# Moving two 128x320 products of a recurrent layer from VectorE to GpSimd, with a new wait on ScalarE

## What is computed

```
y_a = (on + bonus) * silu(g_rwkv)          # silu(g) = g * sigmoid(g)
on  = (o - mean) * rsqrt(var + eps) * ln_w + ln_b
```

## Time and profile before

| | us |
|---|---|
| median of 3 runs | 1145.81 |
| lowest, highest | 1145.09, 1146.93 |
| the profiled execution, its time | 1146.05 |
| the profiled execution, its span | 1144.5 |

### The profile page before, as it was taken

How to read it: one execution, slowest core, us unless ns; L and a number is a source line. 1 busy time by engine, 2 the same in 40 slices (tenths; PEclk the granted TensorE clock), 3 DMA queues, 4 the chain that set the end, 5 groups by cost and what they waited for, 6 DMA issues and landing times.

```text
span 1144.5 us, 23678 instructions
## 1 busy us (share of the span) xinstructions
PE 1117.6 (98%) x8594; PEld 1072.2 (94%) x8594; DVE 794.6 (69%) x1681; ACT 543.7 (48%) x960; POOL 159.7 (14%) x273
## 2 busy tenths in 40 slices
PE   5999999999999999999999999999999999999998
PEld 5889998999999999999999999999999999989998
DVE  5979897979798888988678544444444497685442
ACT  5444747566574747474643333333333343354342
POOL 2422131314131221221140000000000500000000
PEclk9999999999999999999999999999999999999999
DMA  9714433434343343443464555555555965516551
GB/s 239 199 38 124 122 104 111 113 110 115 110 128 97 107 127 99 115 121 103 129 184 130 152 147 154 153 144 149 147 148 147 283 186 148 149 54 167 168 161 38
DMA packets 279708, 155.10 MB, mean 136 GB/s; under 512 B 7717, under 2 KB 275661, under 8 KB 279012
## 3 DMA queue, kind: packets, MB, share of 16 engines
q1 hardware_dynamic: 272528, 139.65, 43.6%
q0 software_dynamic: 6992, 14.87, 4.9%
q10 hardware_dynamic: 148, 0.04, 0.0%
HBM read 149.15 MB, written 5.61 MB: 135 GB/s over the span
## 4 chain that ended last, share of the span: by engine, by line
PE 70%; DVE 17%; issue 6%; DMA 4%; ACT 3%; DVEq 0%; SPq 0%; ACTq 0%; POOL 0%; POOLq 0%
PE acc L1753 14%; PE acc L1755 13%; PE acc L1754 13%; PE wide L1755 6%; PE wide L1754 6%; PE wide L1753 6%; PE wide L1777 4%; DVE wl L1116 3%; PE wide L1860 2%; PE wide L2157 2%; DVE rn L1221 1%; PE wide L1772 1%; DMA wraw<-in_w_out 1%; ACT wh L719 1%; DVE kkn L1511 1%
## 5 line engine op out<-in xcount | busy, mean ns | idle before, releaser
L1116 DVE TENSOR_TENSOR wl<-wraw,wh 128x1024 fp32r<-128x1024 f32 x256 | 315.8, 1240 | 168.6 <-ACT wh L719 166.5
L719 ACT CAST wh<-wraw 128x1024 fp32r<-128x1024 f32 x256 | 266.8, 1048 | 213.3 <-PE acc L1755 124.0
L1753 PE MATMUL acc<-hh,wh 128*128 128x320 f32 (+1 forms) x1084 | 349.4, 322 | 8.6 <-DVE rS L1132 5.6
L1754 PE MATMUL acc<-hl,wh 128*128 128x320 f32 (+1 forms) x1084 | 336.5, 310 | 0.0
L1755 PE MATMUL acc<-hh,wl 128*128 128x320 f32 (+1 forms) x1084 | 335.8, 310 | 0.0
L1753 PEld LDWEIGHTS acc<-hh,wh 128*128 128x128 f32 x1084 | 204.2, 188 | 13.1 <-issue 7.4
L1754 PEld LDWEIGHTS acc<-hl,wh 128*128 128x128 f32 x1084 | 204.1, 188 | 0.3
L1755 PEld LDWEIGHTS acc<-hh,wl 128*128 128x128 f32 x1084 | 204.1, 188 | 0.0
L1753 PE MATMUL acc<-x1h,wh 128*128 128x320 f32 x256 | 81.0, 316 | 0.0
L1753 PE MATMUL acc<-mh,wh 128*128 128x320 f32 x256 | 79.4, 310 | 0.2 <-DVE wl L1116 0.2
L1755 PE MATMUL acc<-x1h,wl 128*128 128x320 f32 x256 | 79.1, 309 | 0.0
(11 more groups left out here) (424 smaller groups left out, 2003.7 us busy)
## 6 DMA issues: line engine op xcount, KB each, us to landing
wraw<-in_w_in SPq DMA_DIRECT2D x160, 512.0 KB, 3.8
wraw<-in_w_branch SPq DMA_DIRECT2D x32, 512.0 KB, 4.0
wraw<-in_w_out SPq DMA_DIRECT2D x32, 512.0 KB, 4.3
wraw<-in_w_ple_gate SPq DMA_DIRECT2D x32, 512.0 KB, 4.2
xt<-in_x_prompt SPq DMA_DIRECT2D x2, 1024.0 KB, 7.2
S0n<-in_state_wkv POOLq DMA_DIRECT2D x64, 32.0 KB, 3.6
out<-so POOLq DMA_DIRECT2D x16, 128.0 KB, 4.1
xt<-in_x_prompt POOLq DMA_DIRECT2D x2, 1024.0 KB, 7.8
```

Source lines behind the costliest of these rows:

```text
L719: A.copy(wh[:, slot, :], wraw[:, slot, :]).then_inc(s["hi_ready"], 1)
L1116: V.tensor_tensor(wl[:, slot, :], wraw[:, slot, :], wh[:, slot, :].bitcast(F32), ALU.subtract).then_inc(s["lo_ready"], 1)
L1753: M.matmul(out[:, 0:width], wh[:, slot, wcol], hi, start=first, stop=False)
L1754: M.matmul(out[:, 0:width], wh[:, slot, wcol], lo, start=False, stop=False)
```

## The change

The product y (L1521) and the product sg (L1305) leave VectorE's queue and are done by GpSimd. On GpSimd sg stands ahead of the copy cur_n and y ahead of the waits for the stores' landing, with a wait for each. ScalarE's second exponential, which overwrites dO, waits until sg is done (and so until the y before it is done), and VectorE's bU, which overwrites sgt, waits for sg.

```diff
 (GpSimd, mix)
                 wait_alone("cur_m_ready", r + 1)
                 wait_alone("acc_free", r * TILES_STEP + (ACC_STEP + TILES_STEP))
+                wait_alone("sg_ready", r + 1)
+                gp_.tensor_tensor(sg[:, :], sgt[:, :], gS[:, :], ALU.mult).then_inc(s["sgs_ready"], 1)
                 gp_.tensor_copy(cur_n[:, :], par[:, LN_W * PAIRS:(LN_B + 1) * PAIRS].rearrange("p (n q) -> p n q", q=PAIRS)
 (GpSimd, mix_out, behind the stores)
+                wait_alone("dve_step", r * 3 + 3)
+                gp_.tensor_tensor(yf[:, ds(r * T, T)], dO[:, :], sg[:, :], ALU.mult).then_inc(s["y_done"], 1)
+
                 wait_alone("eout", r * 32 + 32)
                 wait_alone("sout", r * 32 + 32)
+                wait_alone("y_done", r + 1)
 (ScalarE, mix)
                 A.activation(pi[:, :], cl[:, :], ACT.Exp, scale=DECAY).then_inc(s["exp_ready"], 1)
+                act.wait_ge(s["sgs_ready"], r + 1)
                 A.activation(pd[:, :], cl[:, :], ACT.Exp, scale=-DECAY).then_inc(s["exp_ready"], 1)
 (VectorE, start of mix)
-                dve.wait_ge(s["sg_ready"], r + 1)
                 dve.wait_ge(s["acc_free"], r * TILES_STEP + (ACC_STEP + TILES_STEP))
-                V.tensor_tensor(sg[:, :], sgt[:, :], gS[:, :], ALU.mult).then_inc(s["sgs_ready"], 1)
 (VectorE, ahead of bU)
+                dve.wait_ge(s["sgs_ready"], r + 1)
 (VectorE, end of mix)
-                dve.wait_ge(s["dve_step"], r * 3 + 3)
-                dve.wait_ge(s["sgs_ready"], r + 1)
-                V.tensor_tensor(yf[:, ds(r * T, T)], dO[:, :], sg[:, :], ALU.mult).then_inc(s["y_done"], 1)
                 out(5)
```

## The result

The changed kernel takes 1160.16 us (median of 4 runs, 1159.23 to 1160.24) against 1145.45 us (4 runs, 1144.85 to 1146.93) before: ratio 1.0125, 95% interval 1.0107 to 1.0142. It is slower, by 14.7 us in the medians. The forecast was 1158.3 us, with a range of 1151.0 to 1163.5. Every line after L603 has another number than before: y is L648, sg L603, pd L861, sq_l L1321, rS L1139.

A forecast was written before the change was run, and what follows sets the result against it. TensorE, busy 98% of the span, was taken to wait at pair boundaries for VectorE's queue. Six boundaries at +2.19 us (+13.1), with -0.4 and -0.2 at the ends, gave +12.5: 1158.3 us, range 1151.0 to 1163.5.

The forecast's parts named there:

- What bounds the kernel: At pair boundaries TensorE waits for VectorE's queue up to rS; each us shorter gives up to 0.95 us a pair.
- without a pause of note: From the pair's boundary to rS, VectorE was said to work with no notable idle time.
- The new order at the boundary: Pair r = 4: y holds kf, sg follows cur_p and waits for wl, pd follows sg; sq_l 2.19 us later.
- The size of a boundary: Each of six boundaries (r = 1 to 6) costs 2.19 us more, +13.1 us together.
- the straight line: GpSimd's 128x320 product takes 0.74 us, between 423 ns for 128 columns and 1048 ns for 512.
- the loop's turn: On GpSimd between y and cur_p, an estimated 0.2 us beside the waits.
- The ends: First pair (r = 0) -0.4 us, last pair (r = 7) -0.2, last y 0, at most +0.5.
- the sum: Six boundaries and the ends together cost +12.5 us, giving 1158.6 against the profiled execution, so 1158.3 us.
- sg gets in before wl: Rival at the boundary, chance 0.18 including no exclusion: +1.11 us a pair, 1151.9 us; without exclusion +1.44, 1153.9.
- the relief of VectorE comes through: Rival, chance 0.06: sg done early enough, the 0.95 us gap before tile 3 goes at six boundaries, 1139.5 us.
- The signs: Pairs r = 1 to 6: late sg, VectorE idle before sq_l, TensorE waiting for sq_l, rS wait staying near 0.8 us.
- The collision rule: VectorE instructions with two SBUF inputs and GpSimd instructions reading SBUF exclude each other; the first to start keeps the port pair.

The follow-up runs named there:

- the kernel with y late: Against the kernel before: both products on GpSimd, sg early behind the stores' issue, y mid next pair, dO in xp1, no ScalarE wait; 1139.24 us, ratio 0.9946.
- the kernel above with y at the boundary: Against the kernel before: both products on GpSimd, sg early behind the stores' issue, y at the boundary, ScalarE waits for y alone; 1144.24 us, ratio 0.9993.

## Why the prediction was right, and where it was off

- **What bounds the kernel**: right. TensorE waits for VectorE's queue between the boundary and rS; lengthening it by 2.52 us a boundary cost 2.56 us a pair, shortening it gave 0.89 (the kernel with y late). The words "without a pause of note" pass over one pause of 0.54 us in the kernel before, in which VectorE waits with the wl at 337.56 for ScalarE's cast wh. That cast stands behind bBD, which waits for VectorE's bU, so it comes earlier or later with VectorE's queue.
- **The new order at the boundary**: right in every step. y held kf, cur_p came behind y and sq, sg was dispatched just behind wl (0.28 us, foreseen 0.33) and was held by it; pd followed sg, and sq_h and sq_l followed pd.
- **The size of a boundary**: 2.56 instead of 2.19 us. Three terms were too small by 0.13 us each: y began 0.28 us after the dO step, not 0.15, which was VectorE's own distance; a product took 0.87, not the 0.74 of the straight line; sg ended 0.74 behind wl, not 0.61. One was too large, the step from sg to pd (0.03 instead of 0.1). Together +0.32, which is the difference of 2.52 to 2.19 but for 0.01. The 0.2 us for the loop's turn had no row behind it: from y's end to cur_p it took 0.72 us instead of 0.63, which made no difference, since cur_p ended behind sq, and sg behind wl, all the same. The estimate from the Trainium skill ("GPSIMD Engine Reference", section 3.1 Elementwise), 0.97 us, was 0.10 too high, where the straight line was 0.13 too low.
- **The ends**: the first pair was not 0.4 us quicker. From VectorE's first scan to kf it took 4.98 us (77.45 to 82.43) instead of 4.83 (78.94 to 83.77): sg, done early there (0.87 us from 78.24), met VectorE's pm product (1.15 instead of 0.49 us), and zr (from 80.70) met t_l (1.26 instead of 0.49). Around the last pair VectorE's and ScalarE's order was as foreseen; from gp to gp it took 59.31 us instead of 59.09.
- **Against the profiled executions** the sum is 13.2 us (1157.7 to 1144.5), with 12.5 foreseen, but this is closer than the terms deserve: the profiled execution of the changed kernel reached its first scan 1.5 us sooner, at 77.45 us. This point moves between 77.13 and 80.07 from kernel to kernel in the traces of the study, and what runs ahead of it is not touched by the change. The medians, 14.7 us apart, are the better measure. The forecast lies 1.9 us below the measured median, and the six boundaries alone cost 2.2 us more than forecast (15.3 against 13.1).
- **The rivals.** That sg gets in before wl was tried with the wait ahead of wl: it gives 1.0078, a loss still. Forecast were 1151.9 to 1153.9 us, 6.1 to 8.1 over the median of before; measured were 9.2 over it (1153.43 to 1144.27), a little more than its price. That the relief of VectorE comes through didn't happen in the change, but does in the kernel with y late. Against that rival the prediction put the chain on GpSimd at 2.6 us without a collision; its own terms, with 0.2 us for an undisturbed cur_p, add up to 3.1 (0.74, 0.63, 0.2, 0.79, 0.74), which speaks against it the more.
- **The signs.** sg's end 4.64 us after gp's start (4 to 4.5 foreseen, so a little late), VectorE's idle time 3.89 (3 to 4), TensorE's wait for sq_l 1.79 (1 to 2): right. The wait for rS stayed near 0.8 where it appears, but it appears four times and not seven; the last section says why.
- **The collision rule**: the Trainium skill ("SBUF — State Buffer", section Who interferes with whom) is borne out: kf, sq, sq_l, ar, the scan and wl, each with two inputs in SBUF, were drawn out or drew out a GpSimd instruction. That gp, with one input in PSUM, stays out of y's way can't be read from the changed kernel: they overlap for 0.12 us only, and y, held until gp's end, would have ended 0.74 us behind it, where it did end (0.75). Two rows of the kernel before show such a pair, a VectorE product with one input in PSUM and a GpSimd copy inside its time, each at its own length:

```profile
282.49 0.48 DVE L1385 TENSOR_TENSOR ARK<-wide,cm 128x320 f32<-128x320 f32 x1
```

```profile
282.60 0.22 POOL L554 COPY cur_m<-par 128x14 f32 x1
```

wide lies in PSUM, cm and par in SBUF. The same kind of small copy, cur_n, was held for a whole us by wl (last section).

## What to carry to other kernels

Before work is moved to an idle engine, ask what stands ahead of it in that engine's queue and who waits for its end: here the wait cost 15 us because it stood in the middle of ScalarE's queue, while both products, put where nobody waits for them and VectorE has little work that they collide with, gain 5. A hazard on a shared tile (dO on pd) can turn a cheap product into a wait on the critical chain; another place for the tile takes the wait away. In every pair read here, GpSimd's work on SBUF and VectorE's work with two inputs in SBUF ran in turn and not side by side, so what is moved has to go to a time, not only to an engine.

## What was not expected of the hardware

**TensorE's clock fell behind some of the new stalls, and it cost nothing.** Stretches of the changed kernel (busy us and instructions of PE, PEld, DVE, ACT and POOL, then the granted clock, DMA share, GB/s), r = 3, then r = 4 twice:

```profile
277.60:281.60 4.00, 3.47 (x45) 3.08 (x46) 3.83 (x9) 2.57 (x7) 0.11 (x1) 1.00 0.00 0
341.60:345.60 4.00, 3.73 (x21) 3.39 (x23) 3.83 (x9) 2.57 (x7) 0.08 (x1) 0.57 0.00 0
345.60:349.00 3.40, 3.40 (x50) 3.31 (x47) 2.82 (x5) 3.36 (x9) 3.27 (x7) 1.00 0.52 147
```

Behind the stall of 1.8 us before the bonus sum the granted clock stayed at full speed (2.4 GHz) in three of the six pairs, as in r = 3; in the other three (r = 1, 4 and 5) it fell to the half (1.2 GHz) for some us, 0.57 in the mean from 341.60 to 345.60 in r = 4, and was back in the next 3.4 us. The matmuls show it: the first behind the stall (L1889, above) took 0.49 us, against 0.41 in r = 3, and those that follow (L1756, at 342.42 and 278.24) took 0.48 against 0.31. What decides in which pairs it falls stays open. The repeated run of the same kernel has drops in the same three pairs. Yet the pairs with a drop take as long as those without (64.02 to 64.07 us): TensorE would have waited 0.8 us for rS, and in those pairs arrives later and doesn't wait. That is why the wait for rS is there four times and not seven.

**A short copy can be held as long as a product.** GpSimd's copy cur_n of two columns, 0.18 us when alone, took 1.18 us in the kernel above with y at the boundary, behind VectorE's wl from 329.71 to 330.93.

**What a held instruction hides.** sg held by wl ended 0.74 us behind it, kf held by y ended 0.36 us behind it; each is 0.13 us less than its own length alone (0.87, 0.49). So a held instruction loses nearly all of the time that it overlaps.
